# Merge-gate projections between the items of the second attention, in a two-block transformer kernel

## The chip, the cores and the metric

The kernel runs on one NeuronCore of one Trainium2 chip, as one program whose instruction order is written out by hand for each engine. The metric is the device time of one execution in microseconds. Three executions of the kernel before were timed; the median counts.

## The reference, cut to what matters

The function is two transformer blocks on 256 tokens of width 1024 (with 256 context tokens in the first), all in fp32. The part around the change is the mixer of the second block: one wide projection of the normed input, compressed keys and values, a sparse attention (NSA, three branches per head, weighted by gates per token) and a second causal attention (MoBA), and the merge of the two by two sigmoid gates.

```python
proj = rms_norm(x, g_mix) @ w_in
(q_n, kc_n, vc_n, ks_n, vs_n, kw_n, vw_n, gate_n,
 q_m, k_m, v_m, gate_a, gate_b) = split(proj)
# q, k: rms norm per head, partial rope on 16 of 64 features, softmax in fp32
# kc, vc = silu((blocks of 32 tokens + pe) @ w1) @ w2      15 blocks for 256 tokens
y_nsa = g0 * attn(q, kc, vc) + g1 * attn(q, ks, vs) + g2 * attn(q, kw, vw)   # 8 heads
y_moba = causal attention of q_m, k_m, v_m                                  # 8 heads
merged = (sigmoid(gate_a) * (y_nsa @ w_up_nsa)
          + sigmoid(gate_b) * (y_moba @ w_up_moba))
x = x + merged @ w_out
```

The sigmoids of `gate_a` and `gate_b` (two projections of 1024 columns) are needed only in `merged`. The `gate_n` projection (24 columns) makes the branch weights g0, g1, g2. At 256 tokens both the selection and the window take in all earlier tokens, so that every branch is causal attention over up to 256 keys.

## The kernel before, in words

**Weight units.** Every weight matrix is cut into units, which all engines walk in one order (`weight_units`, L49). A unit of 1 MB is 8 k-tiles of 128 rows by 256 columns. SyncE loads it into one of two raw buffers `w_raw` (L399). ScalarE rounds it to fp32r (`w_hi`, L1334), VectorE takes the rest (`w_lo`, L828), each in two halves; then TensorE multiplies it in three parts (high by high, high by low, low by high) with the activations: 2 x 8 x 3 = 48 matmuls of 256 columns in `feature_unit` (L477) or 48 in `token_unit` (L491). All buffers are double, so that unit u+2 is split when unit u is done and its DMA starts when unit u-2 of it is split. On ScalarE and VectorE `turn_of(u)` empties the PSUM of unit u and makes the second half of unit u+2; `high_ahead(u)` and `low_ahead(u)` make the first half of unit u+3. Semaphores join the engines (`unit_done`, `evac`, `hi_made`, `lo_made`). What stands between two such calls on an engine runs beside the unit that TensorE is at.

**The second block's mixer.** The input norm ends in `between(5, 6, h2)`: squares, sums over partitions on TensorE (L445), a root on ScalarE (L1382), spreading (L452). In the middle of it ScalarE issues eleven DMAs (`second_loads`, L1573): five for the compression weights (4 MB, into buffers that are free by then) and six small ones. Then `projections()` runs 20 units: `w_in_a` (8: queries, keys, the input of the key compression), `w_in_b` (2), `w_in_c` (2: values) and `w_in_d` (8: the merge gates, with the sigmoid as they are evacuated, L1470). The attention's preparation runs beside the last ten of them: branch logits (L623) and their sigmoid, squares and row sums of queries and keys (`row_squares`, `sum_rows` L637), the reciprocal root, spreading it back (`spread_rows` L659, `normalise_rows` L1150), the angles and sines, the swap for the rope (L668), the rotation (`rotate2`, with the cosine part on GpSimd, L1733), the flattening of the compression's input (L1140), the compression itself (`compress`, L647: 16 matmuls each for keys and values, with the 30 block columns as stationary and 256 hidden columns streaming), turning its hidden layer (`turn_hidden`), its second layer (L683, L687) and the norm and rope of the compressed keys (`kc`, L1215 to L1228).

**The attention.** `attention(att2)` has 64 items. An item is one head, one tile of 128 queries and one branch: 16 of 15 keys (compressed), 24 of 128 keys and 24 of 256. TensorE makes scores (L562), VectorE adds the mask and takes the maximum (L1031), and makes the bias (L1038), ScalarE takes the exponential and the sum (L1530), VectorE the reciprocal (L1047) and the product (L1060, L1062), TensorE turns the probabilities (L571), ScalarE copies them (L1543), TensorE multiplies them by the values (L583). TensorE's step s is scores(s), turn_probs(s-3), outputs(s-5), 69 steps in all. Scores use three PSUM banks in turn, turned probabilities three others. After four heads' items of a tile, ScalarE and VectorE keep it as high and low parts (L1549, L1070). TensorE waits for the whole preparation ahead of the first item and for the last kept tile behind the last item. Then `up_phase` (L744) projects both outputs, four units, and VectorE merges them with the gates (L1237 to L1248); `w_out` follows.

The functions that the change touches:

Of the kernel before, what the change touches and what calls it, by code (L numbers as in the profile page):

```python
# [12 lines left out]
P = 128  # L13
D = 1024
NC = D // P
S = 256
# [128 lines left out]
def build(nc, t, out, vec_at):  # L145
# [70 lines left out]
    hid_t = sb("hid_t", [30, 2, S], F32, early2)  # L216
# [106 lines left out]
    Attention = namedtuple("Attention", "items hid b kept closed")  # L323

    def attention_plan(items, hid, b, kept):
        closed, n = [], 0
        for it in items:
            closed.append(n)
            n += it.close
        return Attention(items, hid, b, kept, closed)  # L330
    att1 = attention_plan(items1, hid1, 0, 0)
    att2 = attention_plan(items2, hid2, len(items1), NC)
    turned = [ps_g[:, 3, :], ps_s[:, 2, :], ps_s[:, 3, :]]

# [4 lines left out]
    loads2_in = sem("loads2_in")  # L339
# [19 lines left out]
        for n in ("n_mult", "n_shift", "n_high", "n_low", "o_scaled", "o_mult", "o_added"))  # L359
# [16 lines left out]
    c_first, c_hidden, c_turned, c_hid_c, c_second = (  # L376
        sem(n) for n in ("c_first", "c_hidden", "c_turned", "c_hid_c", "c_second"))
    kc_copied, vc_copied, kc_squared, kc_summed, kc_var, kc_std, kc_step, kc_swapped, kc_made = (
        sem(n) for n in ("kc_copied", "vc_copied", "kc_squared", "kc_summed", "kc_var", "kc_std", "kc_step",
                         "kc_swapped", "kc_made"))  # L380
    merge_a, merge_sum, merge_hi, merge_lo = (sem(n) for n in ("merge_a", "merge_sum", "merge_hi", "merge_lo"))
# [40 lines left out]
    def tensor_program():  # L422
# [40 lines left out]
        def feature_unit(u, acts, kc, mt, ready=None, beside=None):  # L463
            w = [w_[u % 2][:, 0:kc * mt * P].rearrange("p (k n) -> p k n", k=kc) for w_ in (w_hi, w_lo)]
            cs = UNITS[u].cols
            for half in range(2):
# [3 lines left out]
                for m in range(mt):  # L470
                    for k in range(half * kc // 2, (half + 1) * kc // 2):
# [4 lines left out]
                        for n, (wp, ap) in enumerate(PARTS):  # L476
                            mm = pe.matmul(ps_g[:, 2 * (u % 2) + m, cs], w[wp][:, k, m * P:(m + 1) * P],  # L477
                                           acts[ap][:, k, cs], start=(k == 0 and n == 0),
                                           stop=(k == kc - 1 and n == 2))
# [75 lines left out]
        def attention(a):  # L555
            N = len(a.items)

            def scores(i):
                it = a.items[i]
                if i >= 3:  # L560
                    pe.wait_ge(i_max, a.b + i - 2)
                pe.matmul(ps_g[:, i % 3, 0:it.n], it.q, it.k, start=True, stop=True).then_inc(i_scores, 1)  # L562

            def turn_probs(i):
                it = a.items[i]
                pe.wait_ge(i_normed, a.b + i + 1)
                if i >= 3:
                    pe.wait_ge(i_copied, a.b + i - 2)
                for k in range(-(-it.n // P)):
                    w = min(P, it.n - k * P)  # L570
                    mm = pe.transpose(turned[i % 3][0:w, k * P:(k + 1) * P],  # L571
# [1344 lines left out]
```

## Time and profile before

| | us |
|---|---|
| three runs: lowest, median, highest | 2459.74, 2462.63, 2464.52 |
| profiled execution, its own time | 2465.48 |
| its span in the trace | 2464.2 |
| TensorE matmuls busy | 2315.4 (94%) |
| VectorE busy | 1482.7 (60%) |
| ScalarE busy | 1068.6 (43%) |
| GpSimd busy | 120.2 (5%) |
| weight units, matmuls of `feature_unit` (L477) with `h` and `w_hi` | 1006.6 |

The profiled execution is 2.9 us above the median of the runs. "Busy" on TensorE means that a matmul was in flight, at whatever clock; PEclk or "clock" is the level of TensorE's clock that was granted, 1.00 for 2.4 GHz and 0.50 for 1.2 GHz. Times count from the start of the span. The second block's mixer lies between 1864 and about 2200 us; of that, the 20 projection units take 1872.5 to 2028.5, and the second attention 2036 to 2169.

### The profile page before, as it was taken

What the parts mean: (1) busy time and instruction counts of PE and PEld (TensorE: products, weight loads), DVE (VectorE), ACT (ScalarE), POOL (GpSimd) and SP (SyncE); (2) the same over time, 40 slices, a digit from 0 to 9 for tenths busy, and PEclk for the clock granted to TensorE, in tenths of its full rate; (3) what the DMA queues carried; (4) which work ended last, traced back from release to release, by engine and by line L of the source; (5) the groups of instructions that cost most, each with busy time, mean ns of one, the idle gap of its engine ahead of it and who ended that gap; (6) DMA issues with size and microseconds to landing.
All of it is one profiled execution on the core that took longest, in us unless ns stands there. A gap on an engine that the chain in (4) does not pass through costs nothing. (4 is left out here: it accounts for less than half of the span.)

```text
span 2464.2 us, 35572 instructions
## 1 busy us (share of the span) xinstructions
PE 2315.4 (94%) x14610; PEld 2031.8 (82%) x14610; DVE 1482.7 (60%) x2461; ACT 1068.6 (43%) x1740; POOL 120.2 (5%) x83
## 2 busy tenths in 40 slices
PE   5999999999899999899999988969997999999997
PEld 3988889998898888898888985569996975588997
DVE  4765775667666676665577655635654544355554
ACT  4522225644652223663222454554544443334443
POOL 1000001100200000100000110010000010000000
PEclk9999999999899999999999987989997995589999
DMA  7555554455344564445555442015655420034553
GB/s 274 183 166 192 192 165 156 154 188 188 120 172 161 198 197 164 157 159 171 197 181 182 154 146 86 1 55 170 238 182 192 147 95 18 1 115 142 190 176 116
DMA packets 70654, 378.21 MB, mean 153 GB/s; under 512 B 7487, under 2 KB 12223, under 8 KB 43867
## 3 DMA queue, kind: packets, MB, share of 16 engines
q1 hardware_dynamic: 67824, 369.91, 43.7%
q10 hardware_dynamic: 2666, 6.02, 0.7%
q8 instruction: 116, 1.90, 0.3%
q14 instruction: 48, 0.39, 0.0%
HBM read 374.85 MB, written 1.05 MB: 153 GB/s over the span
## 5 line engine op out<-in xcount | busy, mean ns | idle before, releaser
L477 PE MATMUL ps_g<-h,w_hi 128*128 128x256 f32 (+1 forms) x4288 | 1006.6, 330 | 13.8 <-DVE h L916 9.8
L828 DVE TENSOR_TENSOR w_lo<-w_raw,w_hi 128x1024 fp32r<-128x1024 f32 (+2 forms) x614 | 689.5, 1124 | 466.0 <-ACT w_hi L1334 465.4
L1334 ACT ACTIVATE w_hi<-w_raw 128x1024 fp32r<-128x1024 f32 (+2 forms) x614 | 593.0, 969 | 626.0 <-PE ps_g L477 525.7
L477 PEld LDWEIGHTS ps_g<-h,w_hi 128*128 128x128 f32 x4288 | 731.3, 193 | 89.2 <-issue 13.6
L477 PE MATMUL ps_g<-h,w_lo 128*128 128x256 f32 (+1 forms) x2144 | 703.8, 328 | 0.0
L477 PE MATMUL ps_g<-hid,w_hi 128*128 128x256 f32 (+1 forms) x2368 | 496.5, 308 | 3.1 <-DVE y L971 2.1
L477 PEld LDWEIGHTS ps_g<-h,w_lo 128*128 128x128 f32 x2144 | 413.5, 193 | 35.6
L477 PEld LDWEIGHTS ps_g<-hid,w_hi 128*128 128x128 f32 x2368 | 387.4, 192 | 26.5 <-DVE w_lo L828 2.6
L477 PE MATMUL ps_g<-hid,w_lo 128*128 128x256 f32 (+1 forms) x1184 | 363.6, 307 | 0.0
L477 PE MATMUL ps_g<-b_h,w_hi 128*128 128x256 f32 x1504 | 276.4, 287 | 7.7 <-DVE b_h L916 7.3
L477 PEld LDWEIGHTS ps_g<-b_h,w_hi 128*128 128x128 f32 x1504 | 236.3, 193 | 10.9 <-issue 10.0
L477 PEld LDWEIGHTS ps_g<-hid,w_lo 128*128 128x128 f32 x1184 | 227.2, 192 | 11.0
L1714 POOL TENSOR_TENSOR ssum<-ssum,sq 128x512 f32<-128x512 f32 x72 | 110.1, 1530 | 2143.8 <-ACT sq L1358 2143.8
L477 PE MATMUL ps_g<-b_h,w_lo 128*128 128x256 f32 x752 | 214.5, 285 | 0.0
L1451 ACT ACTIVATE gate_tmp<-ps_g 128x256 f32<-128x256 f32 (+1 forms) x146 | 65.5, 449 | 324.6 <-PE ps_g L477 324.6
L953 DVE TENSOR_TENSOR prod<-gate_tmp,ps_g 128x256 f32<-128x256 f32 (+1 forms) x130 | 66.9, 515 | 191.2 <-ACT gate_tmp L1451 191.2
L792 DVE CUSTOM_DVE_ANT_0 ps_s<-mod_raw,cond_b,vecs 128x1024 f32<-128x1024 f32 x128 | 164.9, 1289 | 1.8 <-DMA mod_raw<-in_w_mod 1.7
L792 DVE CUSTOM_DVE_ANT_0 mod_raw<-mod_raw,cond_b,vecs 128x1024 f32<-128x1024 f32 x128 | 164.0, 1281 | 0.0
L477 PEld LDWEIGHTS ps_g<-b_h,w_lo 128*128 128x128 f32 x752 | 144.9, 193 | 0.0
L445 PE MATMUL ps_s<-mats,ssum 128*128 128x1 f32 x192 | 33.6, 296 | 81.5 <-POOL ssum L1714 81.5
L445 PEld LDWEIGHTS ps_s<-mats,ssum 128*128 128x128 f32 x192 | 32.0, 252 | 85.5 <-POOL ssum L1714 67.8
L1481 ACT ACTIVATE hid<-prod 128x256 fp32r<-128x256 f32 (+1 forms) x108 | 54.2, 502 | 22.5 <-DVE prod L953 21.6
(238 smaller groups left out, 1856.1 us busy)
## 6 DMA issues: line engine op xcount, KB each, us to landing
w_raw<-in_gu SPq DMA_DIRECT2D x130, 1024.0 KB, 4.9
mod_raw<-in_w_mod SPq DMA_DIRECT2D x128, 512.0 KB, 3.7
w_raw<-in_conv_cu SPq DMA_DIRECT2D x16, 1024.0 KB, 4.9
w_raw<-in_dn00b SPq DMA_DIRECT2D x16, 768.0 KB, 4.2
w_raw<-in_dn01b SPq DMA_DIRECT2D x16, 768.0 KB, 4.2
w_raw<-in_dn10b SPq DMA_DIRECT2D x16, 768.0 KB, 4.3
w_raw<-in_conv_out SPq DMA_DIRECT2D x8, 1024.0 KB, 4.9
w_raw<-in_w_in_a SPq DMA_DIRECT2D x8, 1024.0 KB, 4.9
```

What stands on the lines that cost most here:

```text
L445: mm = pe.matmul(ps_s[:, s, S + j:S + j + 1], pair_of(ssum, s)[:, a, j * P:(j + 1) * P], ones[:, 0:1], start=(a == 0), stop=(a == 1))
L477: mm = pe.matmul(ps_g[:, 2 * (u % 2) + m, cs], w[wp][:, k, m * P:(m + 1) * P], acts[ap][:, k, cs], start=(k == 0 and n == 0), stop=(k == k ...
L792: return dve.tensor_tensor_reduce(into, w, cond_b[:, s, :], 1.0, b_mod[:, g, s:s + 1], ALU.mult, ALU.add, mod_sb[:, g, s:s + 1])
L828: dve.tensor_tensor(w_lo[u % 2][:, cols], w_raw[u % 2][:, cols], w_hi[u % 2][:, cols].bitcast(F32), ALU.subtract).then_inc(lo_made, 1)
L953: dve.tensor_tensor(prod[:, j, cs], gate_tmp[:, j, cs], ps_g[:, 2 * j + 1, cs], ALU.mult).then_inc(evac, 1)
L1334: act.activation(w_hi[u % 2][:, cols], w_raw[u % 2][:, cols], ACT.Copy).then_inc(hi_made, 1)
L1451: act.activation(gate_tmp[:, j, cs], ps_g[:, 2 * j, cs], ACT.Silu if ph[:2] == "gu" else ACT.Copy).then_inc(gate_made, 1)
L1481: act.activation(hid[0][:, ul, cs], prod[:, j, cs], ACT.Copy).then_inc(half_hi, 1)
L1714: pool.tensor_tensor(ssum[:, s, :], ssum[:, s, :], sq[:, s, :], ALU.add).then_inc(sq_added[s], 1)
```

## The change

Units `w_in_d[1:]`, seven of the eight gate units, are issued on TensorE between thirds of attention steps. The order of the units stays the same. To this end:

- a gate unit writes both its column tiles into one PSUM bank (`gates_at`), the attention's scores go from three banks to two (`scored`), the turned probabilities from three to two (`turned`);
- `attention` on TensorE returns a function for one third of a step (scores, turning or outputs); `attend` is called ahead of each group of three matmuls, from half way through the second gate unit on. 207 thirds are spread over 104 groups;
- on VectorE and ScalarE `beside_gates` puts the evacuation and the splits of the gate units behind given steps (`step_by`);
- the whole preparation is moved forward beside the first twelve units and the first gate unit; the small loads (six) are issued after the norm, the five for the compression after the second unit;
- the compression is computed the other way round, with the weights stationary and the 30 block columns streaming (64 matmuls instead of 32), which makes `turn_hidden` and one copy unnecessary;
- the gates are copied raw and their sigmoid is taken in `up_phase` (`sigmoids`), before each merge.

```diff
@@ attention on TensorE @@
-            for s in range(N + 5):
-                if s < N:
+            def third_of_step(n):
+                s, third = divmod(n, 3)
+                if third == 0 and s < N:
                     scores(s)
-                if 0 <= s - 3 < N:
+                if third == 1 and 0 <= s - 3 < N:
                     turn_probs(s - 3)
-                if 0 <= s - 5 < N:
+                if third == 2 and 0 <= s - 5 < N:
                     outputs(s - 5)
-            pe.wait_ge(i_kept, a.kept + a.items[-1].tile + 1)
+            return third_of_step
@@ scores and turned banks @@
+    att1 = attention_plan(items1, hid1, 0, 0, [ps_g[:, j, :] for j in range(3)],
+                          [ps_g[:, 3, :], ps_s[:, 2, :], ps_s[:, 3, :]])
+    att2 = attention_plan(items2, hid2, len(items1), NC, [ps_g[:, j, :] for j in range(2)],
+                          [ps_s[:, 2, :], ps_s[:, 3, :]])
+    D_UNITS = phase_units("w_in_d")
+    STEPS3 = 3 * (len(items2) + 5)
+    CHUNK0 = 2 * NC // 2
+    CHUNKS = 2 * NC * (len(D_UNITS) - 1) - CHUNK0
+    def step_by(n, chunk):
+        return -(-(2 * NC * (n - 1) + chunk - CHUNK0) * STEPS3 // (3 * CHUNKS)) + 1
+    def gates_at(u):
+        return ps_g[:, 3 - u % 2, :].rearrange("p (m n) -> p m n", m=2)
@@ compress @@
-            if kv:
-                pe.wait_ge(c_hidden, 1)
-            for jp in range(16):
-                mm = pe.matmul(ps_s[0:30, 1, 0:S], flat[:, kv, jp, :, :].rearrange("p g c -> p (g c)"),
-                               compress_w(kv, jp), start=(jp == 0), stop=(jp == 15))
+            pe.wait_ge(cw1_in, 16 * 5)
+            for m in range(2):
+                for jp in range(16):
+                    mm = pe.matmul(ps_s[:, 1, 60 * kv + 30 * m:60 * kv + 30 * m + 30],
+                                   compress_w(kv, jp)[:, m * P:(m + 1) * P],
+                                   flat[:, kv, jp, :, :].rearrange("p g c -> p (g c)"),
+                                   start=(jp == 0), stop=(jp == 15))
@@ projections on TensorE @@
+            for u in a[:3]:
+                feature_unit(u, h2, NC, 2, normed(6, X) if u == a[0] else None)
             branch_matmuls()
+            feature_unit(a[3], h2, NC, 2)
+            feature_unit(a[4], h2, NC, 2)
             sum_rows(range(4))
+            feature_unit(a[5], h2, NC, 2)
             branch_turn()
+            feature_unit(a[6], h2, NC, 2)
+            feature_unit(a[7], h2, NC, 2)
             sum_rows(range(4, 7))
+            feature_unit(b[0], h2, NC, 2)
             pe.wait_ge(br_copied, 1)
             spread_rows((0, 1, 2), 0)
+            compress(0)
+            token_unit(b[1], h2)
+            spread_rows((3, 4, 5), 6)
             compress(1)
+            token_unit(c[0], h2)
             spread_rows((6,), 12)
             swap((0, 1), 1, 12, 0)
             compress_second()
+            token_unit(c[1], h2)
+            kc_sum()
             swap((2, 3, 4), 0, 14, 2)
+            feature_unit(D_UNITS[0], h2, NC, 2, one_bank=True)
+            kc_swap()
             swap((5, 6), 0, 14, 5)
+            third_of_step = attention(att2)
+            def attend(chunk):
+                if chunk == 0:
+                    pe.wait_ge(kc_made, 1)
+                    pe.wait_ge(r_rotated, 7)
+                    pe.wait_ge(br_made, 1)
+                if chunk >= 0:
+                    for n in range(chunk * STEPS3 // CHUNKS, (chunk + 1) * STEPS3 // CHUNKS):
+                        third_of_step(n)
+            for n, u in enumerate(D_UNITS[1:]):
+                feature_unit(u, h2, NC, 2, None, lambda at, n=n: attend(2 * NC * n + at - CHUNK0), one_bank=True)
@@ ScalarE @@
+        def beside_gates(step_):
+            for n, u in enumerate(D_UNITS):
+                if 0 < n < len(D_UNITS) - 1:
+                    if step_ == step_by(n, 2 * NC):
+                        turn_of(u)
+                    if step_ == step_by(n + 1, NC):
+                        high_ahead(u)
+        def sigmoids(ul):
+            for tiles in (slice(2 * ul, 2 * ul + 2), slice(NC + 2 * ul, NC + 2 * ul + 2)):
+                ins = act.activation(gates[:, tiles, :], gates[:, tiles, :], ACT.Sigmoid)
+            ins.then_inc(gates_made, 1)
...
         beside("v0123", 5, 6, X, h2)
-        second_loads()
         sqrt_ready()
         beside("Vabcd", 5, 6, X, h2)
         high_put_off(last_of("dn3b"))
+        second_loads()
         projections()
-        attention(att2)
-        high_ahead(last_of("w_in_d"))
+        attention(att2, beside_gates)
+        turn_of(D_UNITS[-1])
+        act.wait_ge(evac, D_UNITS[-1] + 1)
+        sigmoids(0)
+        high_ahead(D_UNITS[-1])
```

On VectorE the same steps move as on ScalarE (`beside_gates` one step later). In the merge phase TensorE's first unit waits for the evacuation of the last gate unit and, ahead of each half, for the kept tiles that it reads.

## Rows read from the trace of the kernel before

**Rows 1.** The page, part 2: granted TensorE clock in 40 slices of 61.6 us

```profile
PEclk9999999999899999999999987989997995589999
```

**Rows 2.** Stretches: us; busy us of PE, PEld, DVE, ACT, POOL; PEclk; DMA share; GB/s

```profile
1872.50:1940.00 67.50, 67.50 (x554) 67.41 (x555) 31.54 (x30) 30.88 (x36) 0.00 (x0) 0.97 0.59 202
...
2060.00:2100.00 40.00, 40.00 (x121) 22.47 (x121) 15.96 (x102) 15.72 (x61) 0.00 (x0) 0.50 0.00 1
...
2168.00:2172.00 4.00, 3.07 (x14) 2.67 (x14) 0.42 (x1) 0.38 (x1) 0.00 (x0) 0.50 0.00 0
2172.00:2176.00 4.00, 4.00 (x31) 4.00 (x30) 0.53 (x1) 1.06 (x1) 0.00 (x0) 0.85 0.00 0
```

**Rows 3.** Stretches: ten us of the first attention

```profile
1590.00:1600.00 10.00, 10.00 (x53) 5.78 (x53) 5.79 (x25) 5.88 (x17) 0.00 (x0) 1.00 0.01 2
```

**Rows 4.** Timeline, PE, second attention: start us, us, engine line op tiles count

```profile
2045.57 0.79 PE L562 MATMUL ps_g<-qk 64*128 64x128 f32 x2
...
2046.29 0.69 PE L571 MATMUL ps_s<-mats,gate_tmp 128*128 128x128 f32 x2
...
2046.91 0.69 PE L583 MATMUL ps_s<-prod,flat 15*64 15x128 f32 x2
...
2047.52 0.60 PE L562 MATMUL ps_g<-small,qk 64*128 64x15 f32 x2
...
2048.06 0.39 PE L571 MATMUL ps_g<-mats,sq 128*15 128x128 f32 x1
...
2048.38 1.12 PE L583 MATMUL ps_s<-prod,v_tok 128*64 128x128 f32 x4
...
2049.43 1.22 PE L562 MATMUL ps_g<-qk 64*128 64x256 f32 x2
...
2050.58 0.47 PE L571 MATMUL ps_s<-mats,sq 128*128 128x128 f32 x1
```

**Rows 5.** Timeline, PE, first attention, items of 512 keys

```profile
1582.96 1.12 PE L562 MATMUL ps_g<-y 64*128 64x512 f32 x2
...
1584.02 0.66 PE L571 MATMUL ps_s<-mats,sq 128*128 128x128 f32 x4
...
1584.60 1.09 PE L583 MATMUL ps_s<-prod,kv_raw 128*64 128x128 f32 x8
...
1585.62 1.12 PE L562 MATMUL ps_g<-y 64*128 64x512 f32 x2
```

**Rows 6.** Timeline, PE: the first scores of the second attention, idle time before

```profile
2036.06 0.60 PE L562 MATMUL ps_g<-small,qk 64*128 64x15 f32 x2 [5.51 <-DVE small L1228]
```

**Rows 7.** Timeline: sums of the mixer's norm, last DMA issue, root

```profile
1864.13 1.78 PEld L445 LDWEIGHTS ps_s<-mats,ssum 128*128 128x128 f32 x8 [10.51 <-POOL ssum L1714]
...
1867.68 0.54 ACTq L1588 DMA_DIRECT2D pos_i<-in_positions  x1
...
1868.37 0.19 ACT L1382 ACTIVATE tok<-tok 128x2 f32<-128x2 f32 x1
```

**Rows 8.** Groups by line, 1860 to 2040: busy us, mean ns; idle before, releaser

```profile
L623 PE MATMUL ps_s<-b_h,gn 128*24 128x256 f32 x24 | 2.9, 278 | 1.3 <-DVE gn L1177 1.3
```

**Rows 9.** Groups by line, 1860 to 2040: the splits of the weights

```profile
L828 DVE TENSOR_TENSOR w_lo<-w_raw,w_hi 128x1024 fp32r<-128x1024 f32 x41 | 50.9, 1241 | 70.7 <-ACT w_hi L1334 70.6
L1334 ACT ACTIVATE w_hi<-w_raw 128x1024 fp32r<-128x1024 f32 x41 | 43.2, 1054 | 37.1 <-PE ps_g L477 28.8 <-PE ps_g L491 8.3
```

**Rows 10.** Timeline, PE: spreading between two units, and the unit behind it

```profile
1983.88 2.85 PE L659 MATMUL ps_s<-rows,from_row 28*128 28x256 f32 x12
1986.67 0.50 PE L477 MATMUL ps_g<-b_h,w_hi 128*128 128x256 f32 x2
```

**Rows 11.** Timeline: the second compression; sums at full clock; the stretch behind the compression

```profile
1992.56 7.09 PE L647 MATMUL ps_s<-y,flat 128*30 128x256 f32 x32
...
677.19 0.97 PEld L445 LDWEIGHTS ps_s<-mats,ssum 128*128 128x128 f32 x8 [1.36 <-POOL ssum L1714]
...
2004.00:2006.00 2.00, 2.00 (x12) 2.00 (x12) 0.00 (x0) 0.00 (x0) 0.00 (x0) 0.52 0.00 0
```

More of the change, by code:

```diff
@@ L329, in attention_plan @@
             n += it.close
[L330 to L333, printed above, removed]
+        return Attention(items, hid, b, kept, closed, scored, turned)
+    att1 = attention_plan(items1, hid1, 0, 0, [ps_g[:, j, :] for j in range(3)],
[10 more added lines that the diff above has]
+        return ps_g[:, 3 - u % 2, :].rearrange("p (m n) -> p m n", m=2)
     consts_in = sem("consts_in")
@@ L558, in scores @@
             def scores(i):
[L559 to L562, printed above, removed]
+                it, banks = a.items[i], len(a.scored)
+                if i >= banks:
+                    pe.wait_ge(i_max, a.b + i - banks + 1)
+                pe.matmul(a.scored[i % banks][:, 0:it.n], it.q, it.k, start=True, stop=True).then_inc(i_scores, 1)
             def turn_probs(i):
-                it = a.items[i]
+                it, banks = a.items[i], len(a.turned)
                 pe.wait_ge(i_normed, a.b + i + 1)
-                if i >= 3:
-                    pe.wait_ge(i_copied, a.b + i - 2)
+                if i >= banks:
+                    pe.wait_ge(i_copied, a.b + i - banks + 1)
                 for k in range(-(-it.n // P)):
                     w = min(P, it.n - k * P)
-                    mm = pe.transpose(turned[i % 3][0:w, k * P:(k + 1) * P],
+                    mm = pe.transpose(a.turned[i % banks][0:w, k * P:(k + 1) * P],
                                       score_slots[i % 4][:, k * P:k * P + w], ident)
@@ L614, in attn_layer @@
             pe.wait_ge(rot_made, 6)
-            attention(att1)
+            third_of_step = attention(att1)
+            for n in range(3 * (len(items1) + 5)):
+                third_of_step(n)
+            pe.wait_ge(i_kept, NC)
             feature_phase("attn_o", hid1, NC, 2)
@@ L669, in swap @@
                           start=True, stop=True).then_inc(r_swapped, 1)
[L671 to L677 removed]
         def compress_second():
[L680 removed]
+            pe.wait_ge(c_hidden, 1)
             for g in range(2):
@@ L1021, in rotate1, with attention @@
             dve.tensor_tensor(dst, dst, m1, ALU.add).then_inc(rot_made, 1)
-        def attention(a):
+        def attention(a, behind=None):
             N = len(a.items)
@@ L1082, in attention @@
                     keep_low(s - 6)
+                if behind is not None:
+                    behind(s)
         def attn_layer():
@@ L1521, in window, with attention @@
                     beside(code, o, i, s, h1)
-        def attention(a):
+        def attention(a, behind=None):
             N = len(a.items)
@@ L1557, in attention @@
                     keep_high(s - 6)
+                if behind is not None:
+                    behind(s)
         def attn_layer():
```

274 lines of the change are left out of this document (139 added, 135 removed).

## The prediction

> **What bounds the kernel now.** I read the page's row of the granted TensorE clock first. It is near full almost everywhere and falls to 0.5 in the two slices that hold the second attention [rows 1]. Then I cut that part of the trace into stretches [rows 2]. From 1872.5 to 1940 TensorE does nothing but projection units: 554 matmuls in 67.5 us, busy throughout, clock 0.97. From 2060 to 2100, inside the second attention, TensorE is again busy without a gap, but at clock 0.50, that is 1.2 GHz, while VectorE is busy 16.0 and ScalarE 15.7 of 40 us. So the bound of this stage is TensorE at its lower level, and the other engines have more than half of their time free. The first attention, with the same three operations on wider items, holds 1.00 [rows 3]. The lower clock is therefore no property of attention as such: it came after the 5.5 us in which TensorE waited for the last of the preparation [rows 6], and the small second items never brought it back. The units that come before and the merge projection that follows run at the upper level soon after they start.
>
> **The attention's own price at both levels.** Read the starts of successive TensorE rows; each operation lasts until the next one starts. At 0.50 [rows 4]: scores take 1.15 us for 256 keys, 0.72 for 128, 0.54 for 15; turning takes 0.62 for two blocks, 0.40 for one (0.22 less, as its row is 0.47 long instead of 0.69), 0.32 for the 15-wide one; outputs take 1.05 for two blocks, 0.61 for one. There are 24, 24 and 16 items of these sizes: 24 x 2.82 + 24 x 1.73 + 16 x 1.47 = 132.7 us, and the stage does take about 132 us. At 1.00 [rows 5] an item of 512 keys takes 1.06 + 0.58 + 1.02. The slope between 128 and 256 keys at half clock is 3.36 ns a key; half of it, times 512, leaves 0.20 of the 1.06 as fixed. In the same way 0.14 of a turn and 0.16 of an output are fixed, and 0.11 us comes with each record. That gives 0.63 + 0.36 + 0.60 for 256 keys, 0.41 + 0.25 + 0.38 for 128, and 0.29 + 0.22 + 0.38 for 15 (two weight loads limit its scores): 24 x 1.59 + 24 x 1.04 + 16 x 0.89 = 77.4 us. **At the upper level the stage is worth 55.3 us less.**
>
> **Does it get the upper level?** Between the items now stand seven units, 336 dense 128x128x256 matmuls. 103 chunks of three (0.35 us each at full clock) are spread over 69 steps, so some 0.5 us of every 1.8 us step is of the kind that brings the clock up and keeps it up in [rows 2], and the rest is what held 1.00 in [rows 3], on smaller items. The long wait ahead goes too. I take 1.00 all through. The Trainium skill (TensorE: Matmul & The Clock Gate, Part 4: PE-mode transpose) speaks against this: a transpose is said not to count as activity and not to get the full clock. By it the stretch might stay at half, the last rival below. The first attention has four transposes in each item and held 1.00, so the trace disagrees for a mix of operations.
>
> **Savings, part by part.**
> - Eleven DMA issues leave the norm's path. ScalarE issues them between the squares and the root: the sums end at 1865.9, VectorE needs 0.2, but the root starts at 1868.37, behind the last issue (1867.68 + 0.54) [rows 7]. It could start at 1866.3: 2.1 us. The six that stay (about 3 us) stand behind the first split, and ScalarE has about half of each unit's time free there.
> - The branch logits no longer wait for their weights: 1.3 us [rows 8].
> - The wait ahead of the attention: 5.5 us [rows 6], now covered by the first half of the second gate unit, 24 x 0.118 = 2.8 us. I leave 2.6 standing: 2.9 us saved (bounds 2.9 and 5.5; one table load less on ScalarE could help).
> - The attention: 55.3.
> - The merge projection starts warm: the cut from 2168 to 2172 is at 0.50, the next at 0.85, so half clock lasts to about 2173 [rows 2]. It starts near 2169.6, 1 us behind the last item; half of 3.5 us is 1.8.
> - The gates' sigmoid now stands in the merge phase, two more passes on ScalarE per unit plus one table load. ScalarE has the time (two splits of 1.05 and a copy in a 5.7 us unit [rows 9]); if not, at most some 2 us. Nothing.
> Together 63.4 us.
>
> **Costs.**
> - Going back and forth between items and chunks. The nearest row is the row-spreading put between two units: twelve records last 2.79 us instead of the 2.66 that the compression's pace of 7.09 / 32 = 0.222 gives, and the first pair behind it takes 0.50 instead of the 0.40 usual there: 0.23 us per return [rows 10, 11]. 103 returns cost at most 24 us. On the other side, a chunk ahead of an item hides the weight load that is the fixed 0.17 us: as low as -18. I take +8.
> - The compression is turned round: before, 64 records of 256 columns at 0.222 [rows 11] = 14.2 us. After, 128 records that load 128x128 weights for 30 columns. The nearest rows are the sums over partitions, one column per load: 0.97 / 8 = 0.121 at full clock [rows 11], 1.78 / 8 = 0.223 at half [rows 7]. So 15.5 to 28.5 us. TensorE's clock already fell to 0.52 once behind a compression and spreading [rows 11], and this form streams even less, so it should fall in part of it, twice, and slow the start of the unit behind. +6 (1.5 to 16).
> - Preparation beside the first twelve units: 4 MB for the compression now land while weights stream, and ScalarE and VectorE have more between splits. The moved work needs its inputs within one unit's time at several places (squares before row sums; rows' reciprocal before the spreading). A split is ready about one unit early, which covers most of it: +2 (0 to 8). Waits of this sort stop everything queued behind them on their engine, the next splits among them.
> - Waits inside the interleaved stretch. Score banks go from three to two, turned banks from three to two: scores of item i need the bias of i-2, turning i needs the copy of i-2. Seven units bring 13 or 14 splits of 1.24 us to VectorE and of 1.05 to ScalarE [rows 9], with seven evacuations of 0.6. VectorE's and ScalarE's shares per step (16 of 40 us at 2.06 us a step: 0.8 us each [rows 2]) and these splits make 1.1 to 1.2 of a 1.8 us step. A late copy has about 1.3 steps of slack, 2.4 us: +3 (0 to 20).
> - The end: the first merge unit waits for the last gate unit's evacuation, about 1 us, as it waited for the last kept tile before. Nothing.
> Together 19 us.
>
> **Sum:** 63.4 - 19 = 44.4 us. Against the profiled run, 2465.5 - 44.4 = 2421.1. That run is 2.9 above the median, so against the median: 2462.6 - 44.4 = **2418 us**.
>
> **Rivals.**
> - *The interleave is nearly free.* For: weight loads overlap matmuls everywhere in the dense stretches. Switches -5, compression +2, waits 1: 63.4 + 2 = 65 saved, 2397. Chance 0.15.
> - *The items are paced by ScalarE and VectorE around each split.* With two banks each, every ScalarE insertion (0.6 + 1.05 in a unit, then 1.05) stops TensorE for its length: 7 x 2.7 = 19 us more. For: the copy of an item already waits for TensorE in the same step, so that ScalarE can't run ahead. Against: the slack above. 25 saved, 2437. Chance 0.17.
> - *TensorE stays at half clock with the gate units inside*, the slower outcome. Place: the interleaved stretch, if it enters at 0.5 and the mix doesn't lift it. Then 55.3 and 1.8 are not saved, 336 matmuls cost another 0.118 each, 39.6, and switches double to 16: 6.3 - 39.6 - 27 = 60 us slower, 2523. It decides from the share of the stretch at 0.50: zero gain at 44 / (44 + 60) = 42%. Against it: the same dense matmuls raised the clock within 4 us at 2172. Chance 0.05 for more than that share, and 0.05 for a smaller share, 2440 to 2460.
> - My forecast, 2408 to 2432: chance 0.58.
>
> **Chances.** A measurement of this kernel can tell about 0.2%, 5 us. Faster 0.92, same 0.02, slower 0.06. The range reaches from the free interleave to the paced one: 2398 to 2442.
>
> **What would show it.** Clock 1.00 between the start of the second attention and the merge phase, with TensorE busy there for about 40 + 77 + 8 us; a wait of 1 to 3 us instead of 5.5 ahead of the first scores; the root 0.3 us behind the sums; a compression of 8 us or, with a dip in the clock, more. Wrong would be: rows of TensorE waiting for a bias or a copy in most steps (second rival), a clock of 0.5 in any 4 us cut of the stretch (third), or TensorE idle for long among the first twelve units.

## The result and the profile after

The changed kernel takes 2510.97 us (median of four runs, 2510.76 to 2511.99) against 2462.52 before: a ratio of 1.0197, with a 95% interval of 1.0184 to 1.0211. It is 48.5 us **slower**, where 44 us faster was predicted. That it is slower is clear of the noise; whether by a full 2 per cent is not, since the interval reaches to both sides of it. The page of after, granted TensorE clock in 40 slices (62.7 us each), to be read against [rows 1]:

```profile
PEclk9999999999999999999999988979979755589999
```

Before, two slices showed the lower level; now three do, and the slice to their left has fallen to 0.7 (the one to their right is at 0.8 as before). The cuts of after that answer to [rows 2] (columns: us; busy us and records of PE, PEld, DVE, ACT, POOL; PEclk; DMA share; GB/s):

```profile
1872.50:1940.00 67.50, 66.14 (x507) 60.95 (x506) 37.07 (x59) 32.66 (x43) 0.00 (x0) 0.98 0.64 228
1940.00:1952.00 12.00, 12.00 (x58) 12.00 (x58) 1.77 (x5) 0.00 (x0) 0.00 (x0) 0.50 0.07 31
1960.00:1976.00 16.00, 16.00 (x76) 16.00 (x76) 1.38 (x4) 0.27 (x1) 0.00 (x0) 0.50 0.19 66
1976.00:2003.00 27.00, 27.00 (x191) 22.58 (x190) 18.71 (x23) 9.74 (x14) 10.78 (x7) 1.00 0.26 83
2003.10:2005.87 2.77, 0.00 (x1) 0.03 (x1) 2.77 (x6) 2.34 (x2) 0.00 (x0) 1.00 0.81 328
2006.00:2007.00 1.00, 1.00 (x8) 0.91 (x8) 0.97 (x4) 0.00 (x0) 0.00 (x0) 0.94 0.04 16
2010.00:2210.00 200.00, 200.00 (x656) 134.78 (x655) 63.24 (x327) 65.36 (x209) 0.00 (x0) 0.50 0.09 32
2212.00:2217.00 5.00, 4.22 (x28) 3.10 (x28) 2.07 (x3) 2.91 (x7) 0.00 (x0) 1.00 0.00 0
```

From 1976 to 2003 the clock is 1.00. Then TensorE has nothing to do for 2.8 us, starts the interleaved stretch, and one microsecond later it stands at 0.50, where it stays for 200 us without a gap in its work, with three gate matmuls behind every two operations of the attention or so. It comes back at about 2211.7 us, 5 us ahead of the merge projection, 7 us behind the last scores (2204.1), as the items run out. The two cuts at 0.50 around 1946 and 1968 are the two compressions with the start of the unit behind each.

The start of that stretch, TensorE alone (start us, us, what, idle time before it):

```profile
2005.87 0.36 PE L578 MATMUL ps_g<-small,qk 64*128 64x15 f32 x2 [2.79 <-DVE qk L1189]
2006.16 0.50 PE L493 MATMUL ps_g<-b_h,w_hi 128*128 128x256 f32 x2
2006.50 0.28 PE L493 MATMUL ps_g<-b_h,w_lo 128*128 128x256 f32 x1
2006.62 0.42 PE L493 MATMUL ps_g<-b_h,w_hi 128*128 128x256 f32 x2
...
2007.90 0.79 PE L493 MATMUL ps_g<-b_h,w_hi 128*128 128x256 f32 x2
2008.49 0.41 PE L493 MATMUL ps_g<-b_h,w_lo 128*128 128x256 f32 x1
```

The wait before the first scores is [rows 6] halved, 2.79 us instead of 5.51, as the prediction had it. The same pair of gate matmuls takes 0.50 us at 2006.16 and 0.79 at 2007.90: the level changed between the two.

Four points on TensorE cut the kernels into stages; the last two columns are experiments told below.

| us | before | after | E1 | B1 |
|---|---|---|---|---|
| first projection matmul starts at | 1872.5 | 1868.7 | 1868.8 | 1863.6 |
| to the first scores of the second attention | 163.6 | 137.2 | 137.6 | 124.8 |
| to the first merge matmul | 133.5 | 211.0 | 120.3 | 120.3 |
| to the end of the span | 294.6 | 292.8 | 293.4 | 293.2 |
| span | 2464.2 | 2509.7 | 2420.0 | 2401.9 |

The attention's stage has taken in 312 gate matmuls and grew by 77.5 us; the stage ahead gave up only 26.4; the other two rows give 3.8 and 1.8. 77.5 - 26.4 - 3.8 - 1.8 = 45.5, the difference of the spans. (Between kernels that are equal up to there, the changed one and the experiments built on it, the first projection starts anywhere from 1862.4 (B2) to 1875.2 us (E11). So stages are compared here, and a total only where it differs by more.)

### The profile page after: what moved, and what is told of

Same layout as the page of the kernel before. It is cut to its first block and busy times, and to the rows that moved or that the text cites. A ratio compares the mean times of both kernels' runs of the same rounds, so it can differ in the third digit from the quotient of the medians.

```text
span 2509.7 us, 35704 instructions
## 1 busy us (share of the span) xinstructions
PE 2362.6 (94%) x14670; PEld 2077.9 (83%) x14670; DVE 1480.8 (59%) x2461; ACT 1064.2 (42%) x1741; POOL 121.0 (5%) x83
## 3 DMA queue, kind: packets, MB, share of 16 engines
HBM read 374.85 MB, written 1.05 MB: 150 GB/s over the span
## 5 line engine op out<-in xcount | busy, mean ns | idle before, releaser
L493 PEld LDWEIGHTS ps_g<-hid,w_hi 128*128 128x128 f32 x2368 | 384.8, 191 | 26.4 <-DVE w_lo L849 2.5
L493 PE MATMUL ps_g<-b_h,w_hi 128*128 128x256 f32 x1504 | 317.9, 314 | 7.7 <-DVE b_h L937 7.3
L493 PEld LDWEIGHTS ps_g<-b_h,w_hi 128*128 128x128 f32 x1504 | 256.1, 209 | 31.1 <-issue 30.0
L493 PE MATMUL ps_g<-b_h,w_lo 128*128 128x256 f32 x752 | 226.9, 302 | 0.0
L493 PEld LDWEIGHTS ps_g<-b_h,w_lo 128*128 128x128 f32 x752 | 157.9, 210 | 0.0
(236 smaller groups left out, 1889.3 us busy)
```

The source lines that it names most:

```text
L493: mm = pe.matmul(at, w[wp][:, k, m * P:(m + 1) * P], acts[ap][:, k, cs], start=(k == 0 and n == 0 and not (one_bank and m)), stop=(k == kc ...
```

## The experiments

Two theories at first. **Entry**: the mix of items and portions of three matmuls holds the upper level if it enters with it, but doesn't bring it back, and the 2.8 us wait lost it. **Mix**: portions of three are too thin, whatever came before. Terms: a *portion* is a run of gate matmuls issued in a row, an *item* is as above, and "the level" is the granted clock, 1.00 or 0.50. Runs with one time only are told without an interval; the kernel before took between 2456.7 and 2467.2 beside them.

**E1, the attention starts behind a whole gate unit** instead of half of one, so that 24 more matmuls cover the wait; six units are interleaved, not six and a half. (The expectations below call this "one unit later".)

```
-    CHUNK0 = 2 * NC // 2
+    CHUNK0 = 2 * NC
```

> The changed kernel, but the first item comes after the whole second gate unit instead of after its half, so that the wait for the preparation (2.8 us of idle TensorE, then clock 0.50) is covered. Theory 'entry' (the clock was lost in that wait, and a mix of items and dense chunks would hold 1.00 once there): 1.00 through the interleaved stretch, some 75 us less than the changed kernel, near 2435. Theory 'mix' (the items between chunks are too thin a load for the upper level, whatever came before): no wait, yet the clock falls to 0.50 within a few us of the first items and stays, near 2506.

2421.3 us. Three cuts: the second compression, the units and rotations behind it, the interleaved stretch:

```profile
1959.50:1973.00 13.50, 13.50 (x64) 13.50 (x64) 2.39 (x7) 0.09 (x1) 0.00 (x0) 0.50 0.24 78
1973.00:2006.40 33.40, 33.40 (x233) 28.98 (x232) 21.54 (x29) 12.36 (x17) 10.79 (x7) 0.95 0.27 94
2006.40:2120.00 113.60, 113.60 (x645) 78.57 (x645) 64.58 (x338) 61.74 (x212) 0.00 (x0) 1.00 0.17 57
```

The first scores now follow the unit without a wait, and the stretch is at 1.00 throughout. "Mix" is false. One constant turns 48 us slower into some 40 faster (38 against the time of the kernel before beside it, 41 against the median above).

**E6, the wait put back by hand** into E1: four (then two) dummy products on VectorE ahead of the last rotation. This tells the wait from the new place of the items.

```
+            for _ in range(4):
+                step(dve.tensor_tensor(ring[3].rearrange("p (a n) -> p a n", a=2), qk[:, 0:2, :],
+                                       rope2[:, 1:2, :].to_broadcast([P, 2, S]), ALU.mult))
             rotate2((5, 6), 0)
```

> The kernel with the attention one unit later, and four dummy products of 128x512 on VectorE (0.68 us each by the trace) ahead of the last rotation, so that TensorE again waits some 2.7 us in front of the first item. Theory 'entry' (the wait loses the upper level and the mix cannot regain it): clock 0.50 from the first items to the end of the interleaved stretch, 2500 to 2520 us. Rival 'order' (the gain came from the new place of the items, not from the absent wait): clock 1.00 as in the run without the dummies, 2421 plus 3, about 2424 us.

> The same with two dummy products: a wait of about 1.4 us. 'Entry' does not say how long a wait must be: either 0.50 and about 2510 us, or 1.00 and about 2423 us; a value between the two would mean that the level changes in the middle of the stretch. I expect 1.00 (waits of about a microsecond occur between units all through the kernel at 1.00). 'Order': 2423 us.

2509.4 us with four, 2424.1 with two. The first scores and one cut of the stretch, with four:

```profile
2008.77 0.36 PE L578 MATMUL ps_g<-small,qk 64*128 64x15 f32 x2 [2.85 <-DVE qk L1189]
...
2100.00:2110.00 10.00, 10.00 (x35) 6.79 (x34) 2.77 (x16) 2.53 (x9) 0.00 (x0) 0.50 0.01 2
```

and with two:

```profile
2009.37 0.36 PE L578 MATMUL ps_g<-small,qk 64*128 64x15 f32 x2 [1.40 <-DVE qk L1189]
...
2100.00:2110.00 10.00, 10.00 (x59) 6.71 (x57) 5.50 (x29) 5.20 (x17) 0.00 (x0) 1.00 0.01 2
```

A wait 1.45 us longer costs 85 us. This is the shown cause of the result: a stall of 2.8 us at this place loses the level, one of 1.4 us does not, and what follows doesn't restore it. Each of these two lengths was run once; the loss behind 2.79 us shows in all four executions of the changed kernel, whose mean clocks are 0.918 to 0.920 (E1: 0.958). Where between 1.4 and 2.8 us the limit lies at this place was not looked for.

**E2 and E8, longer portions, the wait kept**: 24 and 12 gate matmuls in a row between the items instead of three. The first portion now stands between the wait and the first scores. The edit of E2 (E8 has 4 in place of each 8; both issue the last group behind the last unit):

```
-                if chunk >= 0:
-                    for n in range(chunk * STEPS3 // CHUNKS, (chunk + 1) * STEPS3 // CHUNKS):
+                if chunk > 0 and chunk % 8 == 0:
+                    for n in range((chunk - 8) * STEPS3 // CHUNKS, chunk * STEPS3 // CHUNKS):
```

> The changed kernel with the same work in coarser portions: 24 dense matmuls (half a gate unit) in a row, then the 16 thirds of steps that belonged among them. 'Mix': what counts is how dense a stretch is by itself, so the clock rises in part of the dense portions and falls in the items: between 0.5 and 1.0 in most cuts, 2470 to 2505. 'Entry': lost at the same wait, stays 0.50 as in the changed kernel, near 2510.

> The changed kernel, its 2.8 us wait kept, with twelve matmuls in a row between the items instead of three. 24 in a row brought the upper level back. Theory: if twelve are enough, 1.00 after the first few portions and about 2417 us; if not, 0.50 and about 2510 us. I lean to enough, 60 to 40, since the run of 24 had risen by its end.

2416.4 and 2420.0 us; for E2 both theories had expected far more, for E8 the guess was right. In E8 the wait of 2.79 us stands at 2004 to 2006.8, and then:

```profile
2006.00:2008.00 2.00, 1.16 (x9) 1.19 (x10) 1.72 (x2) 0.50 (x1) 0.00 (x0) 0.94 0.47 197
2008.00:2012.00 4.00, 4.00 (x17) 3.41 (x17) 1.82 (x13) 1.39 (x6) 0.00 (x0) 0.50 0.00 0
2012.00:2016.00 4.00, 4.00 (x20) 3.18 (x20) 1.41 (x10) 0.67 (x4) 0.00 (x0) 0.68 0.00 0
2016.00:2020.00 4.00, 4.00 (x25) 2.80 (x24) 2.33 (x16) 1.98 (x10) 0.00 (x0) 1.00 0.00 0
```

The level falls here too, 0.9 us into the first portion, but is back within some 8 us of the wait's end and stays at 1.00 in every cut of 10 us to the end. In E2 it lasts through the 24 matmuls behind the wait, falls in the first items at about 2007.8 us and is back at about 2011.2. What the prediction claimed for portions of three, that dense matmuls between the items bring the clock back, is true for twelve.

**E3 and E5, what the interleave itself is worth.** E3 puts all gate units ahead of the attention. E5 does the same, but fills the attention's pipeline beside the last unit, so that it starts without a wait (there `attend` issues one third of a step per chunk; VectorE's and ScalarE's calls for these units move with it, which the cut below leaves out):

```
-            for n, u in enumerate(D_UNITS[1:]):
-                feature_unit(u, h2, NC, 2, None, lambda at, n=n: attend(2 * NC * n + at - CHUNK0), one_bank=True)
+            for u in D_UNITS[1:-1]:
+                feature_unit(u, h2, NC, 2, one_bank=True)
+            feature_unit(D_UNITS[-1], h2, NC, 2, None, attend, one_bank=True)
+            for n in range(2 * NC, STEPS3):
+                third_of_step(n)
```

> The changed kernel with its moved preparation, but all gate units in a row and the attention behind them, so that it starts with no wait, from the upper level. 'Entry': the attention alone then runs at 1.00 in 77 us instead of 133: 2463 - 9 + 20 - 55, near 2418. 'Mix': the small items lose the level by themselves in a few us: attention 130 us at 0.50, near 2475; the extra over the kernel before is the slower compression.

> Six gate units ahead of the attention, its first steps (16 thirds) beside the last gate unit so that the pipeline fills without a wait, the other items alone. If the items alone hold the upper level once they enter with it, as the first attention does: 1.00 to the end and about 2415 to 2425 us, the interleave itself worth nothing. If only a mix with dense matmuls holds it: the clock falls to 0.50 within the items, and the time is that of all units ahead of the attention, about 2465 us.

2468.8 and 2463.8 us. E3 waits 2.53 us for its first results, between the second and the third of its scores, and is at 0.50 from there on (2040 us), so it can't tell the wait from the missing matmuls. E5 can:

```profile
2042.00:2044.00 2.00, 2.00 (x13) 1.22 (x12) 1.35 (x10) 1.33 (x7) 0.00 (x0) 1.00 0.00 0
2044.00:2046.00 2.00, 2.00 (x11) 1.11 (x11) 1.74 (x6) 1.58 (x4) 0.00 (x0) 0.91 0.00 0
2046.00:2048.00 2.00, 2.00 (x8) 1.41 (x9) 1.49 (x11) 1.22 (x6) 0.00 (x0) 0.50 0.00 0
```

Its last dense matmuls end at 2042; no wait follows, TensorE is busy, and the level falls 3 to 4 us later. The items of the second attention on their own don't hold it. So the gain of E1 needs both: no long wait ahead, and matmuls (or, as E9 and E11 will show, more work of another kind) among the items.

**E7 and E10, turning by ordinary matmuls.** The prediction named one objection to the mix, its transposes. Here the second attention's probabilities are multiplied by the identity instead: E7 in the changed kernel, E10 in E6 with four dummies (`a.b == 0` is the first attention).

```
-                    mm = pe.transpose(a.turned[i % banks][0:w, k * P:(k + 1) * P],
-                                      score_slots[i % 4][:, k * P:k * P + w], ident)
+                    if a.b == 0:
+                        mm = pe.transpose(a.turned[i % banks][0:w, k * P:(k + 1) * P],
+                                          score_slots[i % 4][:, k * P:k * P + w], ident)
+                    else:
+                        mm = pe.matmul(a.turned[i % banks][0:w, k * P:(k + 1) * P],
+                                       score_slots[i % 4][:, k * P:k * P + w], ident, start=True, stop=True)
```

> The changed kernel with the probabilities of the second attention turned by an ordinary matmul with the identity instead of a transpose; entry with the same wait. If transposes do not count as activity and are what keeps the level down, the clock rises in the interleaved stretch and the time falls to about 2430 us or below. By 'entry' it stays at 0.50 and the turns cost more: a fp32 matmul of 128 columns in place of each transpose, some 0.1 to 0.4 us at half clock for 88 of them, 2515 to 2550 us.

> The kernel one unit later with four dummy products (wait of 2.85 us, 0.50 through the whole stretch, 2509 us), the turning now by ordinary matmuls. If without transposes the mix brings the upper level back by itself, the clock rises inside the stretch here too, at another item than in the first such run (2474 us, risen at 2099 us) or at the same: 2425 to 2480 us. If that rise was chance, 0.50 to the end and about 2509 us.

2474.1 and 2486.5 us; E7 lies between the two outcomes expected for it. Both enter at 0.50 behind the same wait. E7 then:

```profile
2096.00:2098.00 2.00, 2.00 (x9) 1.68 (x9) 0.84 (x5) 0.60 (x2) 0.00 (x0) 0.50 0.00 0
2098.00:2100.00 2.00, 2.00 (x8) 1.18 (x6) 0.00 (x0) 1.33 (x3) 0.00 (x0) 0.64 0.02 4
2100.00:2102.00 2.00, 2.00 (x13) 1.54 (x12) 1.01 (x6) 1.47 (x5) 0.00 (x0) 1.00 0.00 0
```

The clock rises by itself after about 96 us, in E10 after about 125 (the cut from 2130 to 2140 has 0.89), and stays up. With transposes it never did in 200 us. Is it the kind of operation? Three runs with the items alone, in which nothing but the turning differs, tell.

**E9 and E11**, both from E5: E9 turns by matmul; E11 issues every transpose twice into the same place.

```
-                    mm = pe.transpose(a.turned[i % banks][0:w, k * P:(k + 1) * P],
-                                      score_slots[i % 4][:, k * P:k * P + w], ident)
+                    for _ in range(1 if a.b == 0 else 2):
+                        mm = pe.transpose(a.turned[i % banks][0:w, k * P:(k + 1) * P],
+                                          score_slots[i % 4][:, k * P:k * P + w], ident)
```

> As the run whose items stand alone behind a filled pipeline, which fell from 1.00 to 0.50 within its items (2464 us), but with the probabilities turned by ordinary matmuls. If the transposes are what pulls the items below what the upper level wants, the clock stays at 1.00 and the time is about 2405 to 2415 us. If it is the small size of all three operations, it falls to 0.50 as before: 2460 to 2470 us.

> The control of the two runs with the items alone: every transpose of the second attention is issued twice into the same place, so that turning a block takes two records, as by matmul, but both are transposes. If it is that transposes count for less than matmuls, the clock falls to 0.50 within the items as with one transpose (2464 us), and the time is that plus 88 more records of some 0.12 to 0.25 us, 2475 to 2490 us. If only the longer work per item counts, 1.00 to the end as with matmuls, about 2425 us.

2425.7 and 2428.2 us, against 2463.8 for E5; from the first scores to the merge 97.1 and 94.4 us, against 135.2. If the level held, E9 was expected at 2405 to 2415 us, E11 at about 2425; it held in both. A cut of each, E9 first; every cut of 5 us of the stage has 1.00 in both:

```profile
2080.00:2090.00 10.00, 10.00 (x56) 6.51 (x56) 5.82 (x39) 6.16 (x24) 0.00 (x0) 1.00 0.00 0
```

```profile
2080.00:2090.00 10.00, 10.00 (x57) 6.08 (x56) 6.23 (x41) 5.62 (x23) 0.00 (x0) 1.00 0.01 2
```

Doubled transposes hold the level as matmuls do. By the Trainium skill (TensorE: Matmul & The Clock Gate, Part 4: PE-mode transpose) they shouldn't count, and E11 should have fallen like E5. So a transpose does count here, and it does get the full clock: from one start to the next, the turn of two 128-blocks by transposes takes 0.62 us at 0.50 [rows 4] and 0.37 in E5 at 1.00. What E9 and E11 share is that each item gives TensorE more to do, 0.58 us for this turn in E11; that this is what holds the level is an inference from the two. E5, then E11:

```profile
2043.91 0.44 PE L587 MATMUL ps_s<-mats,gate_tmp 128*128 128x128 f32 x2
2044.28 0.43 PE L599 MATMUL ps_s<-prod,v_tok 128*64 128x128 f32 x2
```

```profile
2083.31 0.66 PE L588 MATMUL ps_s<-mats,gate_tmp 128*128 128x128 f32 x4
2083.89 0.43 PE L600 MATMUL ps_s<-prod,v_tok 128*64 128x128 f32 x2
```

To read E7 as a proof against transposes was premature; only the control told it. Redundant work made the kernel 36 us faster, its stage 41.

**B4**, the kernel before with the matmul turning and nothing else:

> The kernel before with one edit: the second attention's probabilities are turned by ordinary matmuls. It enters at 0.50 after its own 5.5 us wait, and its items stand alone. With matmuls instead of transposes the items alone hold 1.00, and the mix brings it back after a long while; whether the items alone bring it back is open. If they do, the clock rises inside the stage and the time is 2410 to 2455 us, by the place where it rises; if not, 0.50 to the end and about 2462 us.

2481.1 us, 19 slower, where the same time was expected, at 0.50 through its whole stage behind its own wait of 5.51 us. The richer items hold the level when they enter with it (E9), but alone don't bring it back; they only cost: the stage grew from 133.5 to 156.9 us, 0.27 us for each of 88 blocks.

**E4, the compression in its old form** (64 records of 256 columns, the hidden layer turned afterwards, with the copies that this needs), all else as in the changed kernel. The edit of the matmuls, cut short:

```
-                    mm = pe.matmul(ps_s[:, 1, 60 * kv + 30 * m:60 * kv + 30 * m + 30],
-                                   compress_w(kv, jp)[:, m * P:(m + 1) * P],
-                                   flat[:, kv, jp, :, :].rearrange("p g c -> p (g c)"),
...
+                mm = pe.matmul(ps_s[0:30, 1, 0:S], flat[:, kv, jp, :, :].rearrange("p g c -> p (g c)"),
+                               compress_w(kv, jp), start=(jp == 0), stop=(jp == 15))
```

> The changed kernel with the compression as before (30 block columns stationary, 256 hidden columns streaming, hidden layer turned afterwards), the rest as changed. Both theories: the two compressions take 7 us each instead of 14, and fewer us behind them are at 0.50, so 14 to 17 us less, near 2496; the interleaved stretch stays at 0.50.

2498.4 us, 12.6 less; the stage from the first projection to the first scores takes 124.7 us instead of 137.2. The two forms, by groups (busy us, mean ns; idle before), first before, then after:

```profile
L647 PE MATMUL ps_s<-y,flat 128*30 128x256 f32 x32 | 7.1, 380 | 0.0
L647 PE MATMUL ps_s<-x,flat 128*30 128x256 f32 x16 | 3.6, 380 | 0.0
L647 PE MATMUL ps_s<-mod_raw,flat 128*30 128x256 f32 x16 | 3.6, 379 | 0.0
```

```profile
L667 PE MATMUL ps_s<-flat,y 128*128 128x30 f32 x64 | 13.7, 397 | 0.0
L667 PE MATMUL ps_s<-flat,mod_raw 128*128 128x30 f32 x32 | 7.1, 396 | 0.0
L667 PE MATMUL ps_s<-flat,x 128*128 128x30 f32 x32 | 5.6, 337 | 0.0
```

14.3 us became 26.4 (28.2 in E1). The new form pulls the clock to 0.50, within 16 records of the first compression and 6 of the second, and the level stays there until the next unit has run for some 3.5 us. Both stand behind 2.8 us of row spreading. In E4 the same spreading with the old form behind it runs at 1.00, with one short dip at the start of the second compression (0.64 and 0.51 in the cuts from 1950 to 1954), which it leaves by itself. The first records of the new form, at 1.00 and behind it:

```profile
1936.69 1.97 PE L667 MATMUL ps_s<-flat,x 128*128 128x30 f32 x16
1938.50 3.51 PE L667 MATMUL ps_s<-flat,mod_raw 128*128 128x30 f32 x16
```

The first 16 take 0.113 us each from start to start. At that pace 128 would take 14.5 us, as long as the old form. So what the new form costs is the level.

**B1, B2, B3, B6, in search of the best version.** B1 is E1 with the old compression. B2 and B3 add to it portions of 24 and of 12 matmuls, B6 the turning by matmul.

> The attention one unit later and the compression in its old form: 2421 minus 12.6 (what the old form took off the changed kernel), about 2409 us; by the terms of my sum for the compression, minus 6, it would be 2415.

> The same with portions of 24 matmuls instead of three. If going back and forth costs something (I took 8 us for 103 returns), fewer changes give 2401 to 2405; if it is free, 2409; if the longer portions delay ScalarE's and VectorE's part of the items, more.

> The fastest kernel so far with portions of 12 matmuls instead of three. With three, the stretch from the first scores to the merge projection took 120.3 us, where its work at full clock is 77.4 for the items and 34.0 for the matmuls: 8.8 us of changes. With 24 the level dropped to 0.50 between portions several times (134.5 us). If twelve keep the runs of items short enough to hold 1.00 and a quarter of the changes is left, the stretch takes 113 to 116 us and the kernel 2398 to 2402; if the level drops here too, 2408 to 2425.

> The fastest kernel so far (one unit later, compression in its old form, 2405 us) with ordinary matmuls in place of the transposes. Its stretch is at 1.00 already, and a turned block takes about as long either way (0.63 against 0.62 us for two blocks at half clock): 2403 to 2408 us.

| run | portions, turning | median us (four runs) | ratio to before, 95% | first scores to merge |
|---|---|---|---|---|
| B1 | 3, transpose | 2405.1 | 0.9750 to 0.9796 | 120.3 |
| B3 | 12, transpose | 2405.9 | 0.9749 to 0.9789 | 114.0 |
| B2 | 24, transpose | 2422.9 | 0.9823 to 0.9862 | 134.5 |
| B6 | 3, matmul | 2416.7 | 0.9800 to 0.9833 | 133.2 |

B1 beats both kernels, 57 us below the one before, and came 4 us below what was expected. B3's stage is 6.2 us shorter, as expected for a quarter of the changes between items and portions. Its total is no better, and 4 us above what was expected: in the profiled executions its first projection starts 5.7 us later than B1's, and its merge phase starts with a dip (0.83 in the cut from 2110 to 2120) behind a wait of 1.05 us. Whether B3 is the better kernel stays open. B2, expected at 2401 to 2405, shows the other edge:

```profile
2020.00:2022.00 2.00, 2.00 (x13) 1.24 (x11) 0.68 (x5) 0.02 (x1) 0.00 (x0) 1.00 0.64 266
2022.00:2024.00 2.00, 2.00 (x12) 1.22 (x13) 1.23 (x7) 1.23 (x5) 0.00 (x0) 1.00 0.00 0
2024.00:2026.00 2.00, 1.87 (x9) 1.17 (x9) 1.46 (x11) 1.83 (x7) 0.00 (x0) 0.71 0.00 0
2026.00:2028.00 2.00, 2.00 (x8) 1.29 (x7) 1.74 (x6) 1.08 (x5) 0.00 (x0) 0.50 0.00 0
```

Between two portions of 24 stand items alone, 6.3 us of them from 2011.2 to 2017.6, in which the level held, and 9.4 us from 2020.6 to 2029.9, in which it fell as in E5, about 4 us after the last dense matmul. It falls seven times in this stage, the first time in the fill, around a wait of 1.76 us. Its waits for ScalarE and VectorE come to 4.2 us. E2, with the same portions and slightly fewer items between them (207 thirds over 13 portions, not 12), held it from 2012 us on; so this size sits at the edge. B6 costs 13.0 us in its stage, 0.15 for each of 88 blocks, where I had expected nothing: I had taken a row of two matmul records (0.63 us at half clock) for two blocks, and it was one.

## Why the prediction was wrong

The step that failed is "I take 1.00 all through" in **Does it get the upper level?** What the runs showed in its place: 0.50 for 200 us behind a wait of 2.79 us, and 1.00 all through as soon as that wait is gone (E1) or half as long (E6). The other steps held, but for two sizes, the compression and the branch logits.

- *Dense matmuls raised the clock within 4 us [rows 2], so portions of three will.* This carried a run of some thirty matmuls over to threes. With twelve it holds (E8), with three it doesn't (after). What three matmuls between the items can do is keep the level (E1), and the prediction took keeping and regaining for one thing. The trace of before had nothing between, which was reason to give the half-clock rival far more than 0.10 in all.
- *The first attention held 1.00 with the same operations [rows 3], so the lower level is no property of attention as such.* Only the second half is right. The 512-key items hold it, the small ones alone lose it from 1.00 (E5). The row of the first attention was the nearest, but not near.
- *A wait of 2.6 us left standing*: measured 2.79. It was priced at its length. It cost the level of the whole stretch: put back by hand into E1, it makes 85 us (E6). The prediction named the 5.5 us wait as the place where before lost its clock and then left half of it standing without asking whether half was enough.
- *Transposes as the objection*: the outcome it warned of came, but by luck: E1 holds 1.00 with the same transposes, and in E11 twice as many help.

**The sizes.** With the level held, E1 is the kernel I had forecast: 2421 against 2418. That closeness is in part luck. Without the wait the sum would have given 2.6 us less, 2416; the compression took 6 us more than its term and the logits' 1.3 us were not saved, while the first projection started 3.7 us earlier where the root explains 2.2, and the interleaved stretch ran 2 us shorter than its terms.
- Items at both levels: 132.7 and 77.4. In after, 312 matmuls at 0.236 make 73.6; 206.3 with the items, measured 211.0. In E1, 288 at 0.118 make 34.0; 111.4 with the items, measured 120.3. So changes between items and portions are left with 4.7 us at half clock and 8.9 at full. The 77.4 was an estimate from wider items, and E9 bears it out: its stage of 97.1 us, less 48 gate matmuls (5.7) and 88 richer turns at 0.15 (13.0, from B6), leaves 78.4. The +8 was right, and doubling it in the half-clock rival was wrong. That rival also charged 336 matmuls, of which 24 stand ahead of the first scores, 2.8 us too much; by the two it (2523) overshot the measured 2511.
- Waits inside the stretch, +3: none showed in after or E1 as TensorE's, nor did the paced rival. They can't be told from the changes' 8.9 us by stages alone.
- Compression, +6 out of 1.5 to 16: measured +12.1 (E4: 12.6 in the time). It was mis-sized because half clock was taken for part of it; it holds for all but the first records.
- Root, 2.1: from the end of the sums to the first projection matmul 6.6 us before, 4.4 after. Right.

The sums' end and the root of after, which answer to [rows 7]:

```profile
1863.78 0.56 PE L460 MATMUL ps_s<-mats,ssum 128*128 128x1 f32 x2
1864.38 0.16 DVE L876 TENSOR_SCALAR tok<-ps_s 128x2 f32<-128x2 f32 x1 [5.42 <-PE ps_s L460]
1864.58 0.20 ACT L1425 ACTIVATE tok<-tok 128x2 f32<-128x2 f32 x1 [3.40 <-DVE tok L876]
```

- Branch logits, 1.3: wrong. The wait is still there. It is for VectorE's half of the split of these weights (L1218), which ran at 1889.3 us, though ScalarE's half had been done since 1883.3: in VectorE's queue it stands behind the split of a projection unit, which came late. The waits of TensorE (total us, times, longest us):

```profile
PE ps_g L578 <- DVE qk L1189: 2.8, 1, 2.8
PE ps_g L493 <- DVE b_h L937: 2.4, 1, 2.4
PE ps_s L643 <- DVE gn L1218: 1.4, 1, 1.4
PE ps_g L769 <- ACT gates L1512: 0.8, 1, 0.8
```

- Preparation beside the first twelve units, +2: the stage ahead of the scores was to be 163.6 - 36.8 (312 matmuls) - 1.3 - 2.9 + 6 + 2 = 130.6 us. Measured 137.2; 6.1 of the difference is the compression, 1.3 the logits, so that of the +2 about 1 is left. Right.
- Gates' sigmoid, nothing: 0.8 us of waiting for the last gates' copy ahead of the merge, as 0.9 for the kept tile before. Right.
- Merge projection at the upper level from its start, 1.8: the last stage is 1.8 us shorter in after, where the level had come back just in time, and 1.2 in E1. Right.

## What to carry to other kernels

Ask of every stall of a few microseconds on TensorE what comes behind it. Ahead of portions of 12 or 24 dense matmuls 2.79 us of it cost its length and 3 to 7 us at the lower level (E2, E8); ahead of a long stretch of small operations it can cost half the clock for all of them, and here 1.45 us more of waiting cost 85. A thin mix that holds the upper level need not be able to regain it: enter it without a wait, or put a dozen matmuls in a row into it every few items. With 24 in a row the items between them can be too many (B2). A busy TensorE says nothing of the level: read the granted clock in short cuts, and try the cheapest shift of the start (here one constant) before judging an interleave.

## What the runs showed of the hardware

- Two histories, one work: the same mix runs for 120 us at 1.00 (E1) or 200 us at 0.50 (after, and E6 with four dummies), by what preceded it. No trace of before could show that.
- Issuing every transpose of the second attention twice (E11) made the kernel 36 us faster, with the level as the reason. What exactly the chip counts isn't settled: more work in each item keeps the level in E9 and E11, and in the mix it brings it back only after 96 and 125 us (E7, E10). No row that was read marks those two moments.
- 128x128 fp32 weights for 30 columns put TensorE at 0.50 within the compression, 26 to 28 us for 128 records where 64 of 256 columns take 14.3, though it is busy without a gap in both. At the pace of their first 16, at 1.00, they would take 14.5.
